# Scores of retention, attention and mLSTM computed for two heads per step, with matmuls of the two partition halves in turn

## The chip, the cores and the metric

The kernel runs on one core of a Trainium2 chip. The metric is the device time of one execution in microseconds (us). The engines are PE (matmuls, with PEld for its weight loads), DVE (vector), ACT (scalar), POOL and SP (which issues most of the large loads). PE writes its results to eight PSUM banks of 512 fp32 columns each, and the other engines read them from there.

## The reference

Two layers, each a hybrid mixer followed by an expert layer (PEER) and a gated embedding. Sequence length 512, width 1024, everything in fp32. The part that matters here is the mixer with its three groups of four heads:

```python
z = (x @ w_in)
ret = retention(q, k, v)               # 4 heads: (q k^T * decay) v, dk 64, dv 128
att = dilated_attention(q, k, v)       # 4 heads of 64: softmax with a count mask
h = mlstm(q, k, v, i, f)               # 4 heads of 64: (q k^T * exp(gates)) v / den
mix = concat(ret * silu(g), att, h * sigmoid(o)) @ w_out
x1 = layer_norm(alpha * x + mix)
y = peer(x1)                           # 16384 experts, 8 heads, top 16 rows of u and v
x = layer_norm(alpha * x1 + y + sigmoid(x1 @ wg + b) * (p @ wp))
```

For every head the scores are products of 64-long vectors. The kernel computes them in whole-sequence form: of the 512 x 512 scores of a head the lower triangle in strips of 512, 384, 256 and 128 columns.

## The kernel before

Each engine runs the same list `MIXER_STEPS` (L69) in order, taking from each step its own share; the list is written out by hand and is the order of the mixer's work on every engine. Semaphores tie the engines together, so an engine that reaches a step too early waits, and everything behind that step on its queue waits with it.

The steps of the list. `ret_qk`, `ret_v`, `att_qk`, `att_v`, `ml_qk`, `ml_vo` and `ret_g` are projections, one block of 128 tokens or columns each (`project`, L1354; `ml_qk` L1423). `ret_s`, `att_s` and `ml_s` are the scores of one head. Their shares:

- `ret_s`: PE makes the four strips (L1436) in three banks, DVE multiplies them by the decay (L1156) into `strips`.
- `att_s`: PE makes four rows of scores (L1460) in three banks: 128 and 384 columns in the first, 256 in the second, 512 in the third (`ROW_BANKS`). DVE adds the mask and takes the minimum (L1196) into `probs`, ACT takes the exponential (L696).
- `ml_s`: PE copies the gate row to all partitions with a matmul over 4 partitions (`pick`, L1479), DVE makes the exponents from it (L1227), ACT takes the exponential (L711), PE makes the strips (L1484), DVE multiplies (L1238).
- `att_tp` transposes the probabilities of a head (PE L1360, ten transposes in three banks; DVE copies them out, L1207). `ret_pv`, `att_pv`, `ml_pv` multiply with the values (L1445, L1474, L1494). After an `ml_pv` DVE divides and takes the head's statistics (L1247 to L807).
- `ml_qk`: after PE, ACT copies the block (L686), DVE convolves it (L1181, L1184), ACT applies the silu.

The q and k of head h lie in the lower 64 partitions when h is even and in the upper 64 when it is odd (`half`). So a score matmul uses one half of the array's rows, and all matmuls of one head use the same half.

`bank_turns` deals the banks: each step has a ring (0: banks 0, 1 and the two halves of `yv`; 1: banks 4, 5 and the two halves of `xps`) and a number of banks, and takes them in turn, four to a ring. `fill` makes PE wait until the previous use of that bank was read:

```python
b, turn = turns[step, i, n]
if turn > 1:
    e.wait_ge(bank_free[b], turn - 1)
```

`ret_s` and `att_s` take three banks of ring 1, `ml_s` four, `att_tp` three of ring 0, a projection one of ring 0, a `pv` one of ring 1.

## Time and profile before

| | |
|---|---|
| median of 3 runs | 3485.58 us (3484.74 to 3487.93) |
| profiled execution, its own time | 3486.61 us |
| its span in the trace | 3484.8 us |
| PE busy | 2974.9 us (85%) |
| DVE busy | 2118.6 us (61%) |
| POOL busy | 1977.5 us (57%) |
| granted clock of PE, mean | 0.972 |

The span falls into two equal layers. In each the mixer comes first (in the first layer up to about 300 us), with little DMA traffic; then the rows of the experts are gathered at around 400 GB/s.
### The profile page before, as it was taken

Reading aid. Unit: us, or ns where it says so; the run is one execution under the profiler, and the core shown is the slowest. Engines: PE = TensorE matmul, PEld = TensorE weight load, DVE = VectorE, ACT = ScalarE, POOL = GpSimd, SP = SyncE. Lnnn points to the kernel's source line nnn. Section 1 sums busy time; section 2 is a strip of 40 time slices with the busy share of each in tenths; the row PEclk is TensorE's granted clock in tenths of the full one; section 3 lists DMA queues with packets and bytes.
Section 4 is the critical chain, followed back from the end, with each engine's and each line's share of the span. In section 5 each row is a group of like instructions: output and inputs, shape, how many; then the busy total and the mean of one; then the engine's idle time right before and its main releaser. Section 6 shows DMA issues by size and latency. Waiting matters only on the chain.

```text
span 3484.8 us, 25951 instructions
## 1 busy us (share of the span) xinstructions
PE 2974.9 (85%) x7760; PEld 1319.7 (38%) x7760; DVE 2118.6 (61%) x4932; ACT 680.2 (20%) x1678; POOL 1977.5 (57%) x2100
## 2 busy tenths in 40 slices
PE   8999888888778979877799998888887799798777
PEld 4655543343223323322246555433432233233222
DVE  1435777776666666775314368776766666667753
ACT  1231211121112212121113313111111122121211
POOL 0002566667766767777400025666777667677774
PEclk9989999999999999999999899999999999999999
DMA  4114999999999999999831149999999999999997
GB/s 144 70 49 139 358 404 405 404 407 395 407 409 396 408 408 401 405 409 409 315 140 49 49 169 363 405 405 405 406 399 407 409 395 408 400 407 406 409 409 301
DMA packets 360801, 1174.44 MB, mean 337 GB/s; under 512 B 36946, under 2 KB 75986, under 8 KB 360404
## 3 DMA queue, kind: packets, MB, share of 16 engines
q0 software_dynamic: 294912, 1073.87, 78.1%
q1 hardware_dynamic: 63284, 98.59, 8.0%
q8 instruction: 62, 1.02, 0.1%
q10 hardware_dynamic: 2464, 0.31, 0.1%
q14 instruction: 79, 0.65, 0.0%
HBM read 1170.54 MB, written 2.10 MB: 336 GB/s over the span
## 4 chain that ended last, share of the span: by engine, by line
PE 41%; DMA 26%; POOL 14%; DVE 9%; issue 6%; ACT 3%; ACTq 0%; DVEq 0%; SPq 0%; POOLq 0%
DMA arena<-in_peer_v,rows 16%; PE bank L1573 12%; DMA arena<-in_peer_u,rows 9%; POOL arena L547 7%; POOL arena L556 7%; PE bank L1381 6%; DVE arena L1044 5%; PE yv L1354 5%; PE bank L1354 4%; PE bank L1534 3%; PE yv L1510 2%; ACT arena L773 1%; PE yv L1423 1%; PE bank L1510 1%; PE bank L1402 1%
## 5 line engine op out<-in xcount | busy, mean ns | idle before, releaser
L1573 PE MATMUL bank<-arena 128*128 128x512 f32 x3904 | 1884.4, 621 | 446.9 <-DMA arena<-in_peer_v,rows 390.1
L1044 DVE CUSTOM_DVE_ANT_0 arena<-arena,xps 128x1024 f32<-128x1024 f32 x1024 | 1241.4, 1216 | 589.3 <-DMA arena<-in_peer_u,rows 543.8
L1573 PEld LDWEIGHTS bank<-arena 128*128 128x128 f32 x3904 | 707.7, 194 | 1607.0 <-DMA arena<-in_peer_v,rows 924.4
L547 POOL DMA_INDIRECT arena<-in_peer_u,rows x1024 | 969.7, 947 | 499.0 <-issue 270.1
L556 POOL DMA_INDIRECT arena<-in_peer_v,rows x1024 | 970.1, 947 | 430.8 <-issue 233.6
L596 ACT ACTIVATE arena<-arena 128x16 f32<-128x16 f32 x64 | 13.9, 218 | 1874.5 <-DVE arena L1044 1874.5
L773 ACT ACTIVATE arena<-keep,arena 128x128 f32<-128x128 f32 x976 | 292.0, 387 | 39.8 <-DVE arena L1069 39.8
L1381 PE MATMUL bank<-xT,arena 128*128 128x128 f32 (+1 forms) x1024 | 229.5, 383 | 3.6 <-DMA arena<-in_peer_wq 2.1
L1381 PEld LDWEIGHTS bank<-xT,arena 128*128 128x128 f32 x1024 | 157.7, 193 | 77.6 <-issue 9.6
L1354 PE MATMUL yv<-arena,xT 128*128 128x512 f32 (+1 forms) x384 | 166.4, 588 | 0.0
L1354 PE MATMUL bank<-arena,xT 128*128 128x512 f32 (+1 forms) x384 | 159.8, 573 | 3.1 <-DMA arena<-in_w_in 2.2
L533 POOL TENSOR_TENSOR arena<-arena,normg 128x256 f32<-128x256 f32 x8 | 5.8, 725 | 193.1 <-ACTq L704 193.1
L1307 DVE TENSOR_TENSOR arena<-arena,bank 128x512 f32<-128x512 f32 x16 | 11.0, 688 | 170.1 <-ACTq L784 152.8
L1534 PE MATMUL bank<-arena,xT 128*128 128x512 f32 x256 | 112.5, 592 | 0.0
L1354 PEld LDWEIGHTS yv<-arena,xT 128*128 128x128 f32 x384 | 74.8, 200 | 80.7 <-issue 79.3
L1354 PEld LDWEIGHTS bank<-arena,xT 128*128 128x128 f32 x384 | 73.8, 195 | 82.5 <-issue 77.4
L529 POOL MEMSET arena<- 128x3 f32 x8 | 0.4, 101 | 151.1 <-PE xps L1445 151.1
L1044 DVE DVE_READ_ACCUMULATOR2_ANT arena<- 128x1 f32 x1024 | 84.6, 83 | 0.0
L1534 PEld LDWEIGHTS bank<-arena,xT 128*128 128x128 f32 x256 | 48.6, 190 | 61.2 <-issue 61.2
L1510 PE MATMUL yv<-arena,xT 128*128 128x512 f32 x160 | 69.6, 592 | 0.0
L524 POOL TENSOR_TENSOR arena<-arena 128x512 f32<-128x512 f32 x8 | 10.1, 1262 | 92.7 <-DVEq L1119 92.7
L537 POOL TENSOR_TENSOR arena<-arena,normg 128x512 f32<-128x512 f32 x8 | 10.1, 1264 | 89.7 <-ACTq L714 89.7
(289 smaller groups left out, 2007.5 us busy)
## 6 DMA issues: line engine op xcount, KB each, us to landing
arena<-in_peer_wq SPq DMA_DIRECT2D x32, 1024.0 KB, 16.5
arena<-in_w_in SPq DMA_DIRECT2D x12, 2048.0 KB, 8.7
arena<-in_peer_u,rows POOLq DMA_INDIRECT x1024, 10.7
arena<-in_peer_v,rows POOLq DMA_INDIRECT x1024, 10.8
arena<-in_w_out SPq DMA_DIRECT2D x4, 2048.0 KB, 7.9
arena<-in_ple_wg SPq DMA_DIRECT2D x4, 2048.0 KB, 21.0
arena<-in_mixer SPq DMA_DIRECT2D x2, 2112.0 KB, 19.1
ln<-in_ln SPq DMA_DIRECT2D x8, 512.0 KB, 8.2
```

Of the source, the lines that this page charges most:

```text
L547: e.indirect_dma_start(urow[i % UR], None, a["peer_u"], bass.IndirectOffsetOnAxis(ap=rows[:, n % RR, k:k + 1], axis=0)).then_inc(u_in[i % ...
L556: e.indirect_dma_start(vrow[i % VR], None, a["peer_v"], bass.IndirectOffsetOnAxis(ap=rows[:, n % RR, k:k + 1], axis=0)).then_inc(v_in[i % ...
L596: e.activation(act_d, dots[:, n % 2, :], ACT.Gelu).then_inc(gelu_done, 1)
L773: e.activation(diag[:, k, :], ident, ACT.Copy, scale=wgt[:, n % 2, k:k + 1]).then_inc(diag_ready, 1)
L1044: e.tensor_tensor_reduce(r, r, xps[:, :], 1.0, 0.0, ALU.mult, ALU.add, dots[:, n % 2, k:k + 1]).then_inc(u_free, 1)
L1354: ins = e.matmul(ps[:, 0:w], xT[:, k, i * P:(i + 1) * P], wt[:, k, :], start=(k == 0), stop=(k == KT - 1))
L1381: ins = e.matmul(ps[:, at:at + hi - lo], wq[m % 2][:, k, n * P:(n + 1) * P], xT[:, k, lo:hi], start=(k == 0), stop=(k == KT - 1))
L1402: ins = e.matmul(ps[:, b * NKEYS:(b + 1) * NKEYS], qT[:, s, b * P:(b + 1) * P], keys[m % KR][:, s, :], start=True, stop=True)
L1423: ins = e.matmul(ps[:, :], wt[:, k, i * P:(i + 1) * P], xT[:, k, :], start=(k == 0), stop=(k == KT - 1))
L1510: ins = e.matmul(ps[:, :], xT[:, k, b * P:(b + 1) * P], wt[:, k % 4, side * 512:(side + 1) * 512], start=(k == 0), stop=(k == KT - 1))
L1534: e.matmul(ps[:, :], xT[:, k, b * P:(b + 1) * P], wg[:, k, :], start=(k == 0), stop=False)
L1573: ins = e.matmul(bank[m][:, :], diag[:, k, :], vrow[i % VR][:, m * 512:(m + 1) * 512], start=(h == 0 and k == 0), stop=(h == PH - 1 and k ...
```

## The change

The scores of two heads are computed in one step. Step `ret_s`, `att_s` or `ml_s` i now stands for heads 2i and 2i+1, so there are two of each per layer and not four. Within a step PE takes a matmul of the even head (lower half of the partitions) and the same one of the odd head (upper half) in turn, each into its own bank. A pair step takes six banks (`ml_s` eight) from the same ring of four. DVE and ACT go through the pair bank by bank, first the even head and then the odd one. The amount of arithmetic is the same. The list of steps is reordered: two projections now stand between scores and their use where one did, and `att_tp` 0 and 1 (2 and 3) follow each other, as do `ret_pv` and `att_pv` of a pair and `ml_pv` 0 and 1.

```diff
-    + [("att_qk", 0), ("ret_s", 0), ("att_qk", 1), ("ret_pv", 0), ("ret_s", 1), ("att_qk", 2),
-       ("ret_pv", 1), ("ret_s", 2), ("att_qk", 3), ("ret_pv", 2), ("ret_s", 3),
-       ("att_v", 0), ("ret_pv", 3), ("att_tr", 0), ("att_tr", 1), ("att_v", 1), ("ret_norm", 0),
+    + [("att_qk", 0), ("ret_s", 0), ("att_qk", 1), ("att_qk", 2), ("ret_pv", 0), ("ret_pv", 1),
+       ("ret_s", 1), ("att_qk", 3), ("att_v", 0), ("ret_pv", 2), ("ret_pv", 3),
+       ("att_tr", 0), ("att_tr", 1), ("att_v", 1), ("ret_norm", 0),
        ("att_tr", 2), ("att_tr", 3), ("att_v", 2), ("att_v", 3), ("gate_cols", 0),
-       ("ml_qk", 0), ("att_s", 0), ("ml_qk", 1), ("att_tp", 0), ("att_s", 1),
-       ("ml_qk", 2), ("att_pv", 0), ("att_tp", 1), ("att_s", 2),
-       ("ml_qk", 3), ("att_pv", 1), ("att_tp", 2), ("att_s", 3),
-       ("ml_vo", 0), ("att_pv", 2), ("att_tp", 3), ("ml_vo", 1), ("att_pv", 3), ("ml_s", 0),
-       ("ml_vo", 2), ("ml_vo", 3), ("ml_pv", 0), ("ml_s", 1),
-       ("ret_g", 0), ("ml_pv", 1), ("ml_s", 2), ("ret_g", 1), ("ml_pv", 2), ("ml_s", 3),
-       ("ret_g", 2), ("ml_pv", 3), ("ml_norm", 0), ("ret_g", 3)]
+       ("ml_qk", 0), ("att_s", 0), ("ml_qk", 1), ("ml_qk", 2), ("att_tp", 0), ("att_tp", 1),
+       ("att_pv", 0), ("att_s", 1), ("ml_qk", 3), ("att_pv", 1), ("ml_vo", 0), ("att_tp", 2), ("att_tp", 3),
+       ("ml_vo", 1), ("att_pv", 2), ("att_pv", 3), ("ml_s", 0),
+       ("ml_vo", 2), ("ml_vo", 3), ("ml_pv", 0), ("ml_pv", 1), ("ml_s", 1),
+       ("ret_g", 0), ("ret_g", 1), ("ml_pv", 2), ("ret_g", 2), ("ml_pv", 3), ("ml_norm", 0), ("ret_g", 3)]
-    "ret_tr": (1, 1), "ret_s": (1, 3), "ret_pv": (1, 1), "att_tr": (1, 1), "att_s": (1, 3),
-    "att_tp": (0, 3), "att_pv": (1, 1), "gate_cols": (1, 1), "ml_s": (1, 4), "ml_pv": (1, 1),
+    "ret_tr": (1, 1), "ret_s": (1, 6), "ret_pv": (1, 1), "att_tr": (1, 1), "att_s": (1, 6),
+    "att_tp": (0, 3), "att_pv": (1, 1), "gate_cols": (1, 1), "ml_s": (1, 8), "ml_pv": (1, 1),
...
+            return i // 2 * 2 * NB + 2 * sum(len(js) for js in ROW_BANKS[:n]) + (1 + i % 2) * len(ROW_BANKS[n])
...
-                        if i >= 2:
-                            e.wait_ge(*step_done("att_tp", i - 2, len(ROW_BANKS) - 1))
+                        if i == 1:
+                            e.wait_ge(*step_done("att_tp", 1, len(ROW_BANKS) - 1))
                         for n, js in enumerate(ROW_BANKS):
-                            src = read(e, step, i, n)
-                            for m, (j, c) in enumerate(js):
-                                w = (j + 1) * P
-                                pr = probs[i % 2][:, ROWS_AT[j]:ROWS_AT[j] + w]
-                                e.tensor_tensor_reduce(pr, src[:, c:c + w], counts[:, SEQ - w:SEQ], -AD ** -0.5, -LOWEST, ALU.add, ALU.min, nmax[:, i, j:j + 1])
-                                e.drain()
-                                e.sem_inc(att_masked, 1)
-                            e.sem_inc(freed(step, i, n), 1)
+                            for z in range(2):
+                                src = read(e, step, i, 2 * n + z)
+                                for m, (j, c) in enumerate(js):
+                                    w = (j + 1) * P
+                                    pr = probs[z][:, ROWS_AT[j]:ROWS_AT[j] + w]
+                                    e.tensor_tensor_reduce(pr, src[:, c:c + w], counts[:, SEQ - w:SEQ], -AD ** -0.5, -LOWEST, ALU.add, ALU.min, nmax[:, 2 * i + z, j:j + 1])
+                                    e.drain()
+                                    e.sem_inc(att_masked, 1)
+                                e.sem_inc(freed(step, i, 2 * n + z), 1)
...
-                            src = read(e, step, i, 1 + n)
-                            for j, c in js:
-                                st = strips[i % 2][:, TRI_AT[j]:TRI_AT[j] + TRI[j]]
-                                done += 1
-                                e.wait_ge(ml_weight, done)
-                                ins = e.scalar_tensor_tensor(st, src[:, c:c + TRI[j]], AD ** -0.5, st, ALU.mult, ALU.mult)
-                            ins.then_inc(freed(step, i, 1 + n), 1)
-                        e.drain()
-                        e.sem_inc(ml_strip, 1)
+                            for z in range(2):
+                                src = read(e, step, i, 2 + 2 * n + z)
+                                for j, c in js:
+                                    st = strips[z][:, TRI_AT[j]:TRI_AT[j] + TRI[j]]
+                                    e.wait_ge(ml_weight, (2 * i + z) * NB + [m for m, _ in sum(TRI_BANKS, ())].index(j) + 1)
+                                    ins = e.scalar_tensor_tensor(st, src[:, c:c + TRI[j]], AD ** -0.5, st, ALU.mult, ALU.mult)
+                                ins.then_inc(freed(step, i, 2 + 2 * n + z), 1)
+                        e.drain()
+                        e.sem_inc(ml_strip, 2)
...
                         for n, js in enumerate(ROW_BANKS):
-                            ps = fill(e, step, i, n)
+                            ps = [fill(e, step, i, 2 * n + z) for z in range(2)]
                             for j, c in js:
-                                ins = e.matmul(ps[:, c:c + (j + 1) * P], half(att_qkT, 0, i, j * P, (j + 1) * P), half(att_qkT, 2, i, 0, (j + 1) * P))
-                            ins.then_inc(filled(step, i, n), 1)
+                                ins = [e.matmul(ps[z][:, c:c + (j + 1) * P], half(att_qkT, 0, 2 * i + z, j * P, (j + 1) * P), half(att_qkT, 2, 2 * i + z, 0, (j + 1) * P)) for z in range(2)]
+                            for z in range(2):
+                                ins[z].then_inc(filled(step, i, 2 * n + z), 1)
...
-                        ps = fill(e, step, i, 0)
-                        e.matmul(ps[:, :], pick[0:H, i, :], gM).then_inc(filled(step, i, 0), 1)
+                        for z in range(2):
+                            ps = fill(e, step, i, z)
+                            e.matmul(ps[:, :], pick[0:H, 2 * i + z, :], gM).then_inc(filled(step, i, z), 1)
                         e.wait_ge(ml_qkT_ready, 4)
                         for n, js in enumerate(TRI_BANKS):
-                            ps = fill(e, step, i, 1 + n)
+                            ps = [fill(e, step, i, 2 + 2 * n + z) for z in range(2)]
                             for j, c in js:
-                                ins = e.matmul(ps[:, c:c + TRI[j]], half(ml_qkT, 2, i, j * P, (j + 1) * P), half(ml_qkT, 0, i, j * P, SEQ))
-                            ins.then_inc(filled(step, i, 1 + n), 1)
+                                ins = [e.matmul(ps[z][:, c:c + TRI[j]], half(ml_qkT, 2, 2 * i + z, j * P, (j + 1) * P), half(ml_qkT, 0, 2 * i + z, j * P, SEQ)) for z in range(2)]
+                            for z in range(2):
+                                ins[z].then_inc(filled(step, i, 2 + 2 * n + z), 1)
```

The edits of `ret_s` on PE and DVE, and those of ACT's exponentials, have the same form; the waits of `att_tp` and `att_pv` on the exponentials count with `pair_rows`.

PE at the first `att_s` of a layer (`ml_qk` is L1423 before and L1432 after, `att_s` L1460 and L1470; the names in brackets are the semaphores waited for, and `bank_free` n says that bank n was read; `yv` and `xps` are two banks each). Before:

```order
L1423 MATMUL bank1<-xT,arena 128x512 [waits bank_free1,w_landed0]
L1423 MATMUL bank1<-xT,arena 128x512 x7
L1460 MATMUL bank5<-arena 128x128 [waits bank_free5,att_qkT_ready]
L1460 MATMUL bank5<-arena 128x384
L1460 MATMUL xps<-arena 128x256 [waits bank_free6]
L1460 MATMUL xps<-arena 128x512 [waits bank_free7]
L1423 MATMUL yv<-xT,arena 128x512 [waits bank_free2]
L1423 MATMUL yv<-xT,arena 128x512 x7
L1360 MATMUL yv<-keep,arena 128x128 [waits bank_free3,att_probs]
```

and now:

```order
L1432 MATMUL bank1<-xT,arena 128x512 [waits bank_free1,w_landed0]
L1432 MATMUL bank1<-xT,arena 128x512 x7
L1470 MATMUL bank5<-arena 128x128 [waits bank_free6,bank_free5,att_qkT_ready]
L1470 MATMUL xps<-arena 128x128
L1470 MATMUL bank5<-arena 128x384
L1470 MATMUL xps<-arena 128x384
L1470 MATMUL xps<-arena 128x256 [waits bank_free4,bank_free7]
L1470 MATMUL bank4<-arena 128x256
L1470 MATMUL bank5<-arena 128x512 [waits bank_free6,bank_free5]
L1470 MATMUL xps<-arena 128x512
L1432 MATMUL yv<-xT,arena 128x512 [waits bank_free2]
L1432 MATMUL yv<-xT,arena 128x512 x7
```

The step ended with the 512-column matmul into a bank of its own; now the two 512-column matmuls go into the banks that the step's first four matmuls have filled, and wait for `bank_free` of both. Two projections follow it, where one and an `att_tp` did.

PE a little later, at `att_tp` (L1360 before, L1369 now) and `att_pv` (L1474, L1483). Before, `att_pv` 0 and `att_tp` 1:

```order
L1474 MATMUL xps<-arena 128x64 [waits bank_free7,att_probsT,att_v_ready]
L1474 MATMUL xps<-arena 128x64 x9
L1360 MATMUL yv<-keep,arena 128x128 [waits bank_free3,att_probs]
L1360 MATMUL yv<-keep,arena 128x128 x3
L1360 MATMUL bank0<-keep,arena 128x128 [waits bank_free0,att_probs]
L1360 MATMUL bank0<-keep,arena 128x128
L1360 MATMUL bank1<-keep,arena 128x128 [waits bank_free1,att_probs]
L1360 MATMUL bank1<-keep,arena 128x128 x3
```

and now, `att_tp` 0 from its second bank on, `att_tp` 1 and `att_pv` 0:

```order
L1369 MATMUL bank1<-keep,arena 128x128 [waits bank_free1,att_probs]
L1369 MATMUL bank1<-keep,arena 128x128
L1369 MATMUL yv<-keep,arena 128x128 [waits bank_free2,att_probs]
L1369 MATMUL yv<-keep,arena 128x128 x3
L1369 MATMUL yv<-keep,arena 128x128 [waits bank_free3,att_probs]
L1369 MATMUL yv<-keep,arena 128x128 x3
L1369 MATMUL bank0<-keep,arena 128x128 [waits bank_free0,att_probs]
L1369 MATMUL bank0<-keep,arena 128x128
L1369 MATMUL bank1<-keep,arena 128x128 [waits bank_free1,att_probs]
L1369 MATMUL bank1<-keep,arena 128x128 x3
L1483 MATMUL xps<-arena 128x64 [waits bank_free7,att_probsT,att_v_ready]
L1483 MATMUL xps<-arena 128x64 x9
```

Both heads' transposes stand together, and the last two banks of the second head are banks 0 and 1 again, which the first head's transposes have filled.

DVE at the first `att_s` (the convolution is L1181, L1184 before and L1189, L1192 now, the masking L1196 and L1205; after each score row comes a short "ISA arena 128x1" that stores its minimum). Before:

```order
L1181 TENSOR_SCALAR arena<-arena,convw 128x512 [waits pad_filled]
L1184 SCALAR_TENSOR_TENSOR arena<-arena,convw 128x512 x3
L1196 ISA arena<-bank5,arena 128x128 [waits bank_full5]
L1196 ISA arena 128x1
L1196 ISA arena<-bank5,arena 128x384
L1196 ISA arena 128x1
L1196 ISA arena<-xps,arena 128x256 [waits bank_full6]
L1196 ISA arena 128x1
```

and now:

```order
L1189 TENSOR_SCALAR arena<-arena,convw 128x512 [waits pad_filled]
L1192 SCALAR_TENSOR_TENSOR arena<-arena,convw 128x512 x3
L1205 ISA arena<-bank5,arena 128x128 [waits bank_full5]
L1205 ISA arena 128x1
L1205 ISA arena<-bank5,arena 128x384
L1205 ISA arena 128x1
L1205 ISA arena<-xps,arena 128x128 [waits bank_full6]
L1205 ISA arena 128x1
L1205 ISA arena<-xps,arena 128x384
L1205 ISA arena 128x1
```

Up to here DVE is in the same place in both; it still convolves the block of `ml_qk` before it reads any score, and then reads four score rows of two heads, where it read two of one, before the first two banks are both free.

## Rows read from the trace of the kernel before

**Rows 1.** The page, part 4: shares of the chain that ended last.

```profile
PE 41%; DMA 26%; POOL 14%; DVE 9%; issue 6%; ACT 3%; ACTq 0%; DVEq 0%; SPq 0%; POOLq 0%
```

**Rows 2.** Stretches: us, busy us (x instructions) by engine, PEclk, DMA share, GB/s.

```profile
150.40:208.00 57.60, 57.60 (x233) 33.50 (x232) 27.67 (x71) 29.13 (x54) 1.45 (x2) 1.00 0.11 37
...
208.00:285.20 77.20, 76.41 (x217) 38.04 (x216) 28.01 (x99) 22.70 (x34) 9.03 (x8) 0.85 0.08 28
...
1945.05:2020.60 75.55, 74.72 (x217) 37.45 (x216) 27.16 (x100) 22.70 (x35) 9.04 (x8) 0.86 0.08 28
```

**Rows 3.** Timeline of PE, retention: start us, us, what, count, idle before.

```profile
87.43 1.99 PE L1436 MATMUL bank<-arena 64*128 64x512 f32 x6
...
89.78 7.13 PE L1354 MATMUL yv<-arena,xT 128*128 128x512 f32 x16
...
99.08 1.99 PE L1436 MATMUL bank<-arena 64*128 64x512 f32 x6
```

**Rows 4.** Timeline of DVE, retention scores.

```profile
89.27 1.35 DVE L1156 TENSOR_TENSOR arena<-bank,arena 128x512 f32<-128x512 f32 x3
...
100.24 0.69 DVE L1156 TENSOR_TENSOR arena<-bank,arena 128x512 f32<-128x512 f32 x1 [1.70 <-PE bank L1436]
```

**Rows 5.** Timeline of PE, attention of the first heads.

```profile
150.37 1.13 PE L1460 MATMUL bank<-arena 64*128 64x128 f32 x4
...
152.72 7.13 PE L1423 MATMUL yv<-xT,arena 128*128 128x512 f32 x16
159.69 0.60 PE L1360 MATMUL yv<-keep,arena 128*128 128x128 f32 x4
...
160.88 1.56 PE L1460 MATMUL bank<-arena 64*128 64x128 f32 x6
```

**Rows 6.** Timeline of DVE, convolution, attention scores, copies of transposes.

```profile
151.77 2.42 DVE L1184 SCALAR_TENSOR_TENSOR arena<-arena,convw 128x512 f32<-128x512 f32 x3
154.35 0.29 DVE L1196 CUSTOM_DVE_ANT_0 arena<-bank,arena 128x128 f32<-128x128 f32 x1 [0.17 <-issue]
...
154.81 0.56 DVE L1196 CUSTOM_DVE_ANT_0 arena<-bank,arena 128x384 f32<-128x384 f32 x1 [0.16 <-issue]
...
155.63 0.42 DVE L1196 CUSTOM_DVE_ANT_0 arena<-xps,arena 128x256 f32<-128x256 f32 x1 [0.25 <-issue]
...
163.70 0.76 DVE L1207 COPY arena<-yv 128x128 f32<-128x128 f32 x2
164.37 1.01 DVE L1207 COPY arena<-bank 128x256 f32<-128x256 f32 x2
```

**Rows 7.** Timelines of PE and ACT around the first `ml_vo`.

```profile
195.59 2.34 PE L1474 MATMUL xps<-arena 128*128 128x64 f32 x20
...
197.51 0.38 ACT L702 ACTIVATE arena<-yv 128x256 f32<-128x256 f32 x1
```

**Rows 8.** Timeline of PE, first `ml_s` and what follows.

```profile
208.00 1.12 PE L1479 MATMUL bank<-arena 4*128 4x512 f32 x2
...
213.36 8.52 PE L1354 MATMUL yv<-arena,xT 128*128 128x512 f32 x16
```

**Rows 9.** Timeline of DVE, first `ml_s`, first `ml_pv`, second `ml_s`.

```profile
209.16 1.68 DVE L1227 SCALAR_TENSOR_TENSOR arena<-bank,arena 128x512 f32<-128x512 f32 x4 [0.63 <-PE bank L1479]
...
232.01 0.16 DVE L1247 COPY arena<-bank 128x4 f32<-128x4 f32 x1 [18.12 <-PE bank L1494]
...
234.79 1.69 DVE L1227 SCALAR_TENSOR_TENSOR arena<-xps,arena 128x512 f32<-128x512 f32 x4
```

**Rows 10.** Stretches of low granted clock, and PE's gap before one.

```profile
209.30:216.10 6.80, 6.80 (x12) 3.00 (x12) 3.42 (x8) 1.92 (x4) 0.00 (x0) 0.50 0.00 0
...
287.80:291.20 3.40, 3.39 (x16) 3.39 (x17) 3.18 (x5) 0.58 (x1) 1.08 (x1) 0.51 0.99 408
...
287.81 1.10 PE L1360 MATMUL bank<-keep,acc 128*128 128x128 f32 x4 [2.61 <-DVE acc L1265]
```

More of the change, by code:

```diff
@@ L1220, in _ @@
                     elif step == "ml_s":
-                        if i >= 2:
-                            e.wait_ge(*step_done("ml_pv", i - 2))
-                        src = read(e, step, i, 0)
-                        for j, _ in sum(TRI_BANKS, ()):
-                            st = strips[i % 2][:, TRI_AT[j]:TRI_AT[j] + TRI[j]]
-                            ins = e.scalar_tensor_tensor(st, src[:, j * P:SEQ], -1.0, causal[:, 0:TRI[j]], ALU.mult, ALU.add)
-                            ins.then_inc(ml_expo, 1)
@@ L1240, in _ @@
-                        e.drain()
-                        e.sem_inc(ml_strip, 1)
+                        if i == 1:
+                            e.wait_ge(*step_done("ml_pv", 1))
+                        for z in range(2):
+                            src = read(e, step, i, z)
+                            for j, _ in sum(TRI_BANKS, ()):
+                                st = strips[z][:, TRI_AT[j]:TRI_AT[j] + TRI[j]]
+                                ins = e.scalar_tensor_tensor(st, src[:, j * P:SEQ], -1.0, causal[:, 0:TRI[j]], ALU.mult, ALU.add)
+                                ins.then_inc(ml_expo, 1)
+                            e.drain()
+                            e.sem_inc(freed(step, i, z), 1)
@@ new lines, in _ @@
+                        for n, js in enumerate(TRI_BANKS):
+                            for z in range(2):
+                                src = read(e, step, i, 2 + 2 * n + z)
+                                for j, c in js:
+                                    st = strips[z][:, TRI_AT[j]:TRI_AT[j] + TRI[j]]
+                                    e.wait_ge(ml_weight, (2 * i + z) * NB + [m for m, _ in sum(TRI_BANKS, ())].index(j) + 1)
+                                    ins = e.scalar_tensor_tensor(st, src[:, c:c + TRI[j]], AD ** -0.5, st, ALU.mult, ALU.mult)
+                                ins.then_inc(freed(step, i, 2 + 2 * n + z), 1)
@@ L1433, in _ @@
                         for n, js in enumerate(TRI_BANKS):
[L1434 removed]
+                            ps = [fill(e, step, i, 2 * n + z) for z in range(2)]
                             for j, c in js:
[L1436 to L1437 removed]
+                                ins = [e.matmul(ps[z][:, c:c + TRI[j]], half(ret_qkT, 2, 2 * i + z, j * P, (j + 1) * P), half(ret_qkT, 0, 2 * i + z, j * P, SEQ)) for z in range(2)]
+                            for z in range(2):
+                                ins[z].then_inc(filled(step, i, 2 * n + z), 1)
                     elif step == "ret_pv":
```

51 lines of the change are left out of this document (25 added, 26 removed).

## The prediction

> **What bounds the kernel now.** I read the chain that ended last, to see whether the mixer counts at all: PE has 41% of it [rows 1]. In the chain's order in time the mixer's pieces are PE's projections, one behind the other, and the gathers of expert rows come only after it, since they need its result. A microsecond in a mixer is one in the kernel, twice, for the two layers.
>
> Then the stretches of the mixer. In the attention part PE is busy for 57.6 of 57.6 us at the full clock, DVE for 27.7 and ACT for 29.1; in the mLSTM part for 76.4 of 77.2 us, but at a granted clock of 0.85 (second layer 0.86) [rows 2]. So PE sets the time, and less PE work would shorten it. The question is whether PE can still run without waiting: it never had to wait for a score bank.
>
> Last, single steps. Four fp32 matmuls of one head (1280 columns) take PE from 87.43 to 89.78, 2.35 us, the same in attention (150.37 to 152.72) [rows 3, 5]. Two heads in turn take 4.70. PE's work for the three mixers' scores is 12 x 2.35 = 28 us of a layer.
>
> **The change, part by part.** All durations are of the profiled execution; its own time, 3486.6 us, is 1.0 above the median of the runs.
>
> *The matmuls.* The trace of before never has matmuls of the lower and the upper half side by side, so the price of a pair is bounded: 4.70 us if they run one after the other, 2.35 plus a short tail if they overlap. I take the overlap, since the two use other rows of the array and other banks, and nothing in the rows excludes it. By this a 512-column pair takes 0.94 us and 0.4 until the second is through, a 256-column pair 0.7.
>
> The Trainium skill, page "TensorE: Matmul & The Clock Gate", section "Part 3: Packing small matmuls", has matmuls in different row groups running at once, with 3.07 times the speed for four of them. No row of this case shows it; by an estimate from that page a pair would lie at the lower of my bounds.
>
> *The banks.* A pair step fills two banks, then two more, and needs the first two again. So PE's last pair of matmuls starts only when DVE has read both of the first banks. That is the new wait, and projections are queued behind it.
>
> `ret_s` 0: PE starts at 87.43 and reaches the last pair 1.9 us later. DVE begins to read at 89.27, because it rotates `att_qk` 0 first [rows 4]; two reads of 0.69 end at 90.65. The last pair ends at 91.4: 4.0 us against 4.70. `ret_s` 1: DVE begins 1.16 after PE (100.24 against 99.08 [rows 3, 4]), is through with both banks at 2.5, PE ends at 3.3. Together **-2.1 us**.
>
> `att_s` 0: DVE convolves the projection just made before it reads a score; it reads the first 3.98 us after PE begins (154.35 against 150.37 [rows 5, 6]). The first bank of a head holds 128 and 384 columns and takes DVE 1.28 us (154.35 to 155.63). Before, PE had gone on by 152.72. Now it needs both first banks: 3.98 + 2 x 1.28 = 6.5, then the 512-column pair, 7.8 us against 4.70: **+3.1**, with PE idle for 5 us in it.
>
> `att_tp` 0 and 1: now behind `ml_qk` 2. DVE convolves that block first and copies the first transposes 4.01 us after the projection's end (163.70 against 159.69), 0.67 for the first bank (to 164.37) and 1.01 for the others [rows 5, 6]. PE makes `att_tp` 0 and the first bank of `att_tp` 1 in 1.6 us and then wants bank 0 again, which is free at 4.7, and bank 1 at 5.1. `att_pv` 0 waits for DVE's last copy of head 0, at 5.85. One `att_tp` took 1.19 (159.69 to 160.88), so it is 5.9 against 2.4: **+3.5**.
>
> `att_s` 1 has no convolution ahead: 1.16 + 2.56 = 3.7, and 1.3 for the last pair, 5.0 against 4.70: **+0.3**. `att_tp` 3 takes the bank of `ml_vo` 0, which ACT gives back when its sigmoid ends at 197.89, 2.3 us after PE's projection (195.59) [rows 7]; PE wants it at 1.15: **+1.2**. Attention in all +8.1.
>
> `ml_s` 0 at full clock: two gate rows, 1.12 each in the trace and some 0.95 when they follow each other, 1.9; DVE begins at 1.16 (209.16 against 208.00) and takes 1.68 for each head [rows 8, 9], so the banks of the gate rows are free at 4.8, where PE has waited since 3.2. Then 1.1 for the second banks, and DVE must read the first two with 0.69 each, until 6.2; end at 6.9. `ml_s` 1 has `ml_pv` 0 and 1 right before it, each 2.8 us of DVE (232.01 to 234.79 [rows 9]) while PE makes one in 2.3: DVE starts 2.3 later, end at 9.2. Together 16.1, against four steps of about 1.05 and 2.35 at full clock, 13.6.
>
> The Trainium skill, page "TensorEngine Tiling (Array Packing)", section "PSUM Bottleneck", speaks against the change in the same way: tiling speeds up TensorE but not the evacuation of PSUM. By that rule alone, with no convolution ahead of DVE, a pair of `att_s` would cost what `att_s` 1 does, +0.3; the rows ask more for `att_s` 0, since DVE is not only slow but late.
>
> *The clock.* After the 64-column matmuls of `att_pv` and the gate row the granted clock goes to 0.50 for 6.8 us and takes the projection behind (8.52 us, against 7.13) with it [rows 5, 8, 10]. Over the mLSTM part this costs 77.2 x 0.15 = 11.6 us in the first layer and 75.55 x 0.14 = 10.6 in the second. Now two such places remain in place of four. In each, about 1.8 us of matmuls and up to 2.5 us worth of projection lie at half clock, 4.3 lost; the rest falls into PE's waits. So 16.1 + 8.6 = 24.7, against 13.6 + 11.6 = 25.2 and 24.2: **about 0**.
>
> A PE gap of 2.61 us ends in 3.4 us at 0.51 [rows 10], 1.7 us lost. The gaps of 5 us in `att_s` 0 and 3.1 us in `att_tp` are new. For the first I take 2.5, between 1.7 (as in that row) and 3.4 (as 6.8 us at 0.50). Behind the second lie `att_pv` 0 with 64-column matmuls (2.34 [rows 7]), another wait of 2.1 in `att_s` 1 and then a projection; bounds are 0, if it doesn't fall, and 6.8, and I take 4.5. Together **+7.0**.
>
> *Work on other engines* (ACT's exponentials, DVE's reads, POOL's) has the same count and is costed at nothing elsewhere: PE has the projections to cover it, 6.97 us each, as before.
>
> Sum per layer: -2.1 + 8.1 + 7.0 + 0 = +13.0; for two, +26. Own time 3486.6 + 26 = 3512.6, less the 1.0: 3511.6, and I say 3511.
>
> **The rivals.**
> 1. *The halves do not overlap.* Each pair then takes its full 4.70. Where DVE sets the pace it hides part of it: retention gives back only 0.3 and not 2.1, attention loses 0.8 more, mLSTM 1.2. That is 3.8 per layer: 3519. For it: no row shows an overlap. A chance of 0.15.
> 2. *The clock stays up in attention.* The waits are there, the falls aren't: 3511 - 14 = 3497. For it: the falls shown in the mixer before came only after the gate rows and after one gap, never among `att_s` and `att_tp`. Against: gaps of 2.6 us already did it. 0.15.
> 3. *The clock stays up in the mLSTM part*, as there are half as many places and both halves work at once in them: 8.6 per layer back, 3494; with rival 2 too, 3480, no change that can be told. 0.12 and 0.04.
> 4. *Faster: PE is not held by the banks.* Six pairs at 2.2 us saved are 13 us a layer, 3459. It decides at one point: DVE must have read both first banks of a pair before PE asks for them, 1.9 us after its start. The rows have 3.2, 2.5, 6.5, 3.7 and, in mLSTM, 4.8. 0.03.
>
> **How the numbers follow.** The forecast has 0.51, and 3503 to 3519 of its own. The range takes in rival 3 below (3494) and rival 1 with both attention falls at 6.8 us, +3.2 a layer, above (3525). A measurement of this kernel tells 0.2%, 7 us, from no change. Slower by that is all above 3492.5: forecast, rivals 1 and 2 and rival 3 but for the lower part of it, 0.88; within 0.2% 0.08; faster 0.04.
>
> **What would show it.** PE's timeline must have a gap of about 5 us before the 512-column matmuls of `att_s` 0 and of 3 us inside `att_tp` 1, ended by DVE, in both layers; in `att_s` 0 the two 128-column matmuls should start apart by less than one of them takes. The attention part should grow from 57.6 to about 72 us, retention shrink by 2, mLSTM stay within 2. PEclk of the attention part should be near 0.9. The forecast is wrong if these gaps are short because DVE reads earlier than its order has it, or if the clock falls for much longer in them.

## The result and the profile after

The changed kernel takes 3504.8 us (median of 6 runs, 3500.2 to 3507.2) against 3486.1 of before (6 runs, 3484.6 to 3489.1). The ratio is 1.0049, with a 95% interval of 1.0039 to 1.0059: it is slower, by 0.5%. Its profiled execution took 3505.7 us, with a span of 3503.8 us against 3484.8, 19.0 more.

The answer to [rows 2], by stretches from the first score of attention in PE's timeline to the first gate row, and from there to the first transpose of the mixed rows. The columns are length, busy us (x instructions) of PE, PEld, DVE, ACT and POOL, PEclk, DMA share and GB/s. First the first layer's attention and mLSTM, then the second layer's attention:

```profile
147.03:220.69 73.66, 62.40 (x234) 35.47 (x233) 27.66 (x71) 25.05 (x51) 1.46 (x2) 0.86 0.08 29
220.69:295.74 75.05, 66.34 (x218) 33.68 (x217) 29.46 (x105) 17.90 (x30) 10.77 (x10) 0.89 0.10 33
1893.20:1967.21 74.01, 62.76 (x233) 35.95 (x233) 27.66 (x71) 25.05 (x51) 1.46 (x2) 0.84 0.08 29
```

Attention takes 73.7 and 74.0 us, where it took 57.6, with the same DVE work and PE idle for 11.3 us of it. The granted clock is 0.86 (0.84 in the second layer), where it was 1.00.

From the starts of steps in the two timelines:

| stretch of PE | before | after, layer 1 | after, layer 2 |
|---|---|---|---|
| first `ret_s` to first `att_tr` | 43.1, 43.1 | 40.5 | 40.5 |
| first `att_tr` to first `att_s` | 19.9, 19.9 | 19.9 | 19.9 |
| first `att_s` to first gate row | 57.6, 57.6 | 73.7 | 74.0 |
| first gate row to first `mix_tr` | 79.8, 78.1 | 75.1 | 73.1 |

Per layer this is -2.6, +16.0 and -4.8, and in the second -2.6, +16.4 and -5.0: +17.5 of the 19.0 us. The other 1.5 lie outside the mixers.

Where the time of attention goes, in PE's timeline after (start, us, what, count, and in brackets the idle time before and what ended it). These rows answer to [rows 5]; the first three show the turns:

```profile
147.03 0.37 PE L1470 MATMUL bank<-arena 64*128 64x128 f32 x1
147.04 0.37 PE L1470 MATMUL xps<-arena 64*128 64x128 f32 x1
147.24 0.27 PE L1470 MATMUL bank<-arena 64*128 64x128 f32 x1
...
153.59 1.19 PE L1470 MATMUL bank<-arena 64*128 64x512 f32 x1 [4.99 <-DVEq L1207]
...
155.60 16.17 PE L1432 MATMUL yv<-xT,arena 128*128 128x512 f32 x32
...
172.26 1.04 PE L1369 MATMUL yv<-keep,arena 128*128 128x128 f32 x8
176.50 1.21 PE L1369 MATMUL bank<-keep,arena 128*128 128x128 f32 x6 [3.20 <-DVE arena L1216]
177.50 4.43 PE L1483 MATMUL xps<-arena 128*128 128x64 f32 x20
181.86 2.08 PE L1470 MATMUL bank<-arena 64*128 64x128 f32 x8
...
186.66 2.08 PE L1470 MATMUL bank<-arena 64*128 64x512 f32 x4 [1.87 <-DVEq L1207]
188.67 8.13 PE L1432 MATMUL yv<-xT,arena 128*128 128x512 f32 x16
...
208.19 0.63 PE L1369 MATMUL yv<-keep,arena 128*128 128x128 f32 x4 [1.20 <-ACT arena L708]
```

The matmuls of the two heads start 10 ns apart: the halves run side by side. The four gaps are 4.99, 3.20, 1.87 and 1.20 us, and 4.98, 3.20, 1.87 and 1.20 in the second layer. After the first the last pair runs at half clock (1.19 us for one MATMUL of 512 columns) and the two projections take 16.01 us (155.60 to 171.61) in place of 13.84. After the second `att_pv` 0 takes 4.36 (177.50 to 181.86) in place of 2.2.

DVE at the first gap, the answer to [rows 6]:

```profile
148.43 2.42 DVE L1192 SCALAR_TENSOR_TENSOR arena<-arena,convw 128x512 f32<-128x512 f32 x3
151.02 0.29 DVE L1205 CUSTOM_DVE_ANT_0 arena<-bank,arena 128x128 f32<-128x128 f32 x1 [0.17 <-issue]
...
152.29 0.29 DVE L1205 CUSTOM_DVE_ANT_0 arena<-xps,arena 128x128 f32<-128x128 f32 x1 [0.25 <-issue]
...
153.57 0.42 DVE L1205 CUSTOM_DVE_ANT_0 arena<-xps,arena 128x256 f32<-128x256 f32 x1 [0.25 <-issue]
```

It convolves first, then reads the first bank of the even head from 151.02 and that of the odd head from 152.29, and goes on to the next bank at 153.57, when both first banks are read. PE starts the last pair at 153.59.

mLSTM, the answer to [rows 8]:

```profile
220.69 1.12 PE L1489 MATMUL bank<-arena 4*128 4x512 f32 x2
...
225.54 0.97 PE L1494 MATMUL bank<-arena 64*128 64x384 f32 x1 [1.82 <-DVEq L1239]
...
228.40 8.74 PE L1363 MATMUL yv<-arena,xT 128*128 128x512 f32 x16
...
249.41 1.12 PE L1489 MATMUL xps<-arena 4*128 4x512 f32 x2
...
256.64 0.97 PE L1494 MATMUL xps<-arena 64*128 64x384 f32 x1 [3.09 <-DVEq L1239]
...
259.50 8.55 PE L1363 MATMUL bank<-arena,xT 128*128 128x512 f32 x16
...
295.74 0.66 PE L1369 MATMUL bank<-keep,acc 128*128 128x128 f32 x4 [2.61 <-DVE acc L1274]
```

### The profile page after: what moved, and what is told of

The parts are those of the page before. It is cut to its first block, busy times and chain, and to the rows that moved or that the text cites. A ratio compares the mean times of both kernels' runs of the same rounds, so it can differ in the third digit from the quotient of the medians.

```text
span 3503.8 us, 25935 instructions
## 1 busy us (share of the span) xinstructions
PE 2963.6 (85%) x7760; PEld 1311.1 (37%) x7760; DVE 2115.1 (60%) x4932; ACT 661.4 (19%) x1664; POOL 1979.2 (56%) x2100
## 4 chain that ended last, share of the span: by engine, by line
PE 38%; DMA 29%; POOL 13%; DVE 10%; issue 6%; ACT 3%; DVEq 0%; ACTq 0%; SPq 0%; POOLq 0%
DMA arena<-in_peer_v,rows 17%; DMA arena<-in_peer_u,rows 11%; PE bank L1584 11%; POOL arena L558 6%; POOL arena L549 6%; PE bank L1390 5%; DVE arena L1051 5%; PE yv L1363 4%; PE bank L1363 4%; PE bank L1545 3%; PE yv L1521 2%; ACT arena L780 2%; PE yv L1432 1%; PE bank L1521 1%; DMA arena<-in_w_in 1%
## 5 line engine op out<-in xcount | busy, mean ns | idle before, releaser
L1363 PE MATMUL yv<-arena,xT 128*128 128x512 f32 (+1 forms) x384 | 157.5, 564 | 0.0
L1089 DVE SCALAR_TENSOR_TENSOR yv<-arena,yv 128x1024 f32<-128x1024 f32 x46 | 59.0, 1284 | 2.3 <-DMA arena<-in_peer_v,rows 1.2
## 6 DMA issues: line engine op xcount, KB each, us to landing
arena<-in_peer_wq SPq DMA_DIRECT2D x32, 1024.0 KB, 16.4
```

What stands on the lines that cost most here:

```text
L1089: e.scalar_tensor_tensor(yv[:, :], vrow[i % VR], w, yv[:, :], ALU.mult, ALU.add).then_inc(v_added, 1)
L1363: ins = e.matmul(ps[:, 0:w], xT[:, k, i * P:(i + 1) * P], wt[:, k, :], start=(k == 0), stop=(k == KT - 1))
```

## The experiments

All are made from the changed kernel or from parts of the change. Every comparison with before is with runs taken beside it; before took 3485.0 to 3487.5 us in these groups, so that a difference between two experiments, or to the changed kernel (beside which before took 3486.1), has 1 to 2 us more of doubt than the intervals say. A "stretch" is always the one of the table above.

### Each mixer's pairs alone

The edit undoes the change in the other mixers: their score steps, banks and part of the list are those of before. For retention alone, against the changed kernel:

```diff
-       ("ml_qk", 0), ("att_s", 0), ("ml_qk", 1), ("ml_qk", 2), ("att_tp", 0), ("att_tp", 1),
...
+       ("ml_qk", 0), ("att_s", 0), ("ml_qk", 1), ("att_tp", 0), ("att_s", 1),
...
-    "ret_tr": (1, 1), "ret_s": (1, 6), "ret_pv": (1, 1), "att_tr": (1, 1), "att_s": (1, 6),
-    "att_tp": (0, 3), "att_pv": (1, 1), "gate_cols": (1, 1), "ml_s": (1, 8), "ml_pv": (1, 1),
+    "ret_tr": (1, 1), "ret_s": (1, 6), "ret_pv": (1, 1), "att_tr": (1, 1), "att_s": (1, 3),
+    "att_tp": (0, 3), "att_pv": (1, 1), "gate_cols": (1, 1), "ml_s": (1, 4), "ml_pv": (1, 1),
```

> The kernel before, with the pair step and the new order for retention alone. Theory (the parts add up, each at what the stage shows in the trace after): PE's stretch from the first score of retention to the first transposes of attention goes from 43.1 to 40.5 us in each layer, and nothing else moves: 5.2 us less than before, ratio 0.9985. Rival (the reordering makes waits that only the whole set shows, or retention gains nothing by itself): ratio 1.000.

Measured: 3479.4 us, ratio 0.9980 (0.9971 to 0.9989). Retention's stretch is 40.5 us in both layers; attention's stays 57.6. The mLSTM stretch of this trace matters for what follows: its steps are those of before, and yet it is 76.4 us in both layers, where before has 79.8 and 78.1.

```profile
205.82:282.25 76.43, 73.03 (x217) 36.59 (x217) 30.28 (x105) 23.29 (x35) 10.76 (x10) 0.89 0.09 31
```

The clock is low for 17.6 and 17.4 us of it, against 23.9 and 20.5 in before (lengths worked out from the granted clock of stretches of 0.5 us). So this part moves by over 3 us per layer with nothing in it changed, and of the 7 us that this kernel gained only 5.2 are retention's for certain.

> The kernel before, with the pair step and the new order for attention alone. Theory (all of the loss is attention's, from waits of PE on score and transpose banks and the clock falls behind them): the attention stretch goes from 57.6 to about 73.8 us in each layer, 32 us more than before, ratio 1.0093. Rival (the loss is spread, or comes from the steps at the seams between the mixers): less than half of that, ratio below 1.005.

Measured: 3523.6 us, ratio 1.0108 (1.0092 to 1.0123), 37 us more. Attention's stretch is 73.7 and 72.8 us, 31 us more in all; of the rest 1 us lies in the mLSTM stretches (80.9 and 78.1), and some 3 to 5 outside the mixers.

> The kernel before, with the pair step and the new order for mLSTM alone. Theory (the gain of 4.8 us per layer that the trace after shows in the mLSTM stretch is the pair's own): 9.7 us less than before, ratio 0.9972. Rival, as the prediction had it (pair steps of mLSTM gain nothing, and the gain seen after was the luck of where the clock fell): ratio 1.000.

Measured: 3477.6 us, ratio 0.9975 (0.9966 to 0.9984). mLSTM's stretch is 74.8 and 73.4 us against 79.8 and 78.1. So the gain was no luck of one trace, and the prediction's 0 for mLSTM was wrong. Its size is less certain than these two pairs of numbers make it look: over all traces kept, the stretch is 76.4 to 80.9 us in the six layers with single heads in mLSTM (mean 78.3), and 72.5 to 75.1 in the sixteen that have pairs with the banks of one ring (mean 73.9). The two sets don't meet, and their means are 4.4 apart.

> Pair steps for retention and mLSTM, attention as before. Theory (additive): 2 x (2.6 + 4.8) = 15 us less than before, 3471 us, ratio 0.9957, faster than both kernels. Rival (the parts interfere): ratio 0.999 or more.

Measured: 3474.3 us, ratio 0.9962 (0.9949 to 0.9976), 12 us less than before and 30 less than the changed kernel. The three single parts, -7, +37 and -9, add up to +21; the whole change has +18.7. So the loss is attention's alone, within what such a comparison tells (some 5 us).

### The waits against the clock

Matmuls of no use were put where PE waits, each group into a bank that PE overwrites later; they change no result.

```diff
+            def extra(step, i, n, count):
+                ps = fill(e, step, i, n)
+                for _ in range(count):
+                    e.matmul(ps[:, :], xT[:, 0, 0:P], xT[:, 0, :])
...
+                            if n == 2:
+                                extra("ml_qk", 2 * i + 1, 0, (5, 2)[i])
...
+                            if (i, n) == (1, 1):
+                                extra("att_s", 1, 0, 3)
```

> The changed kernel, with matmuls of no use put where PE waits: five 512-column matmuls before the last pair of att_s 0, two in att_s 1 and three before the second bank of att_tp 1, each group into a bank that PE overwrites later. The waits themselves are the same length or a little less. Theory (about 8 us per layer of the loss are projections and attention matmuls at 1.2 GHz behind these gaps): the granted clock of the attention stretch stays at 1.0, 8 us per layer less, 3489 us. Rival (the clock is low because matmuls of the halves or of 64 columns keep it low, gaps or not; or it costs little, since DVE holds PE anyway): 3503 us or more.

Measured: 3489.6 us, ratio to before 1.0010 (1.0001 to 1.0019), 15 us less than the changed kernel with ten matmuls more per layer. Attention's stretch in the first layer (it is 65.6 in the second too), and pieces of it in PE's timeline (the added matmuls are L1376; five of the program show as x10):

```profile
147.13:212.70 65.57, 62.95 (x254) 34.56 (x253) 27.69 (x71) 24.94 (x51) 1.45 (x2) 1.00 0.09 33
```

```profile
148.63 4.56 PE L1376 MATMUL yv<-xT 128*128 128x512 f32 x10
153.69 0.66 PE L1478 MATMUL bank<-arena 64*128 64x512 f32 x1 [0.51 <-DVEq L1207]
...
154.75 14.00 PE L1438 MATMUL yv<-xT,arena 128*128 128x512 f32 x32
...
174.42 2.42 PE L1493 MATMUL xps<-arena 128*128 128x64 f32 x20
```

The clock stays at 1.00, the projections take 13.84 us and `att_pv` 0 2.34. PE still can't start the last pair before 153.69, 6.6 us after the step's start, as in the changed kernel. So of attention's +16.0 us, 8.1 are the clock (73.66 less 65.57), and 7.9 the waits (65.57 less 57.63), less what the pairs save in matmuls; in the second layer 8.5 and 7.9. The rival is out: neither the half-row matmuls nor those of 64 columns keep the clock low in this stretch when the gaps are filled.

### The banks

The third pair of banks of `att_s` comes from ring 0, in `bank_turns`; no order is changed.

```diff
+RINGS_OF = {"att_s": (1, 1, 1, 1, 0, 0)}
...
         for j in range(n):
+            ring = RINGS_OF.get(step, (ring,) * n)[j]
             turns[step, i, j] = (4 * ring + used[ring] % 4, used[ring] // 4 + 1)
```

> The changed kernel, with the third pair of banks of att_s taken from ring 0, so that no bank of the step is used twice in it; the order of steps is unchanged. Theory (PE waits for the first banks to be read): PE's gaps of 5.0 us in att_s 0 and 1.9 in att_s 1 are gone, and with the first of them the clock fall that costs 3.1 us; 9 to 11 us per layer less, 3484 us. Rival (DVE is the pace of the stage, and PE waits as long elsewhere, at att_tp or the next projection): 3500 us or more.

Measured: 3483.2 us, ratio to before 0.9987 (0.9978 to 0.9996); attention's stretch is 62.1 and 62.3 us. PE's rows at `att_s` 0 (the pair began at 147.98), and at `att_tp`:

```profile
149.39 1.02 PE L1474 MATMUL yv<-arena 64*128 64x512 f32 x4
150.34 14.00 PE L1436 MATMUL bank<-xT,arena 128*128 128x512 f32 x32
...
169.07 1.51 PE L1373 MATMUL yv<-keep,arena 128*128 128x128 f32 x6 [3.20 <-DVE arena L1220]
170.38 4.37 PE L1487 MATMUL bank<-arena 128*128 128x64 f32 x20
...
176.54 2.61 PE L1474 MATMUL bank<-arena 64*128 64x256 f32 x8
```

A whole pair step takes 2.36 us at full clock, what one head took before, and the gap of 5 us is gone. The gap in `att_s` 1 is gone too. That in `att_tp` stays at 3.20 and takes the clock down as before. So to take the third pair of banks of `att_s` from the step's own ring cost 21.6 us, waits and the low clock behind them together, more than the 18.7 that the whole change lost.

### The transposes

```diff
-       ("ml_qk", 0), ("att_s", 0), ("ml_qk", 1), ("ml_qk", 2), ("att_tp", 0), ("att_tp", 1),
-       ("att_pv", 0), ("att_s", 1), ("ml_qk", 3), ("att_pv", 1), ("ml_vo", 0), ("att_tp", 2), ("att_tp", 3),
-       ("ml_vo", 1), ("att_pv", 2), ("att_pv", 3), ("ml_s", 0),
+       ("ml_qk", 0), ("att_s", 0), ("ml_qk", 1), ("att_tp", 0), ("ml_qk", 2), ("att_tp", 1),
+       ("att_pv", 0), ("att_s", 1), ("ml_qk", 3), ("att_pv", 1), ("ml_vo", 0), ("att_tp", 2),
+       ("ml_vo", 1), ("att_tp", 3), ("att_pv", 2), ("att_pv", 3), ("ml_s", 0),
```

> The changed kernel, with a projection between att_tp 0 and att_tp 1, and between att_tp 2 and att_tp 3, as it was before; pairs of scores are kept. Theory (transposes of the second head wait for DVE's copies of the first): PE's gaps of 3.2 and 1.2 us there are gone, but att_s 1 now has DVE's convolution and copies ahead and waits some 2 us longer; net 2.5 us per layer less in waits, and up to 5 more if the clock stays up, 3490 to 3500 us. Rival (the new order of att_tp costs nothing, all comes from the scores' banks): within 2 us of the changed kernel.

Measured: 3494.0 us, ratio 1.0022 (1.0012 to 1.0031), 11 us less than the changed kernel. Attention's stretch is 67.5 and 68.3 us. The new place of `att_tp` costs some 6 us per layer (73.7 less 67.5, 74.0 less 68.3). The gap of 5.0 us in `att_s` 0 is still there. That of 3.20 is gone, that of 1.20 became one of 1.11 before `ml_vo` 1, and `att_s` 1 now waits 2.15 and 1.46 us in place of 1.87. The four waits are 1.5 us shorter in sum; the rest is the clock, which is low for 10.2 and 13.7 us, where it was for 20.5 and 23.9.

### DVE's lateness

```diff
-       ("ml_qk", 0), ("att_s", 0), ("ml_qk", 1), ("ml_qk", 2),
+       ("att_s", 0), ("ml_qk", 0), ("ml_qk", 1), ("ml_qk", 2),
```

> The changed kernel, with att_s 0 ahead of ml_qk 0 in the list, so that DVE reads the scores before it convolves. Theory (in att_s 0 it is mostly DVE's lateness, 3.98 us with the convolution against 1.16 without, that makes PE wait for the banks): PE's gap in att_s 0 falls from 5.0 to about 2.2 us, 2.8 us per layer less, and up to 3.1 more if the clock stays up: 3493 to 3499 us. Rival (the convolution then comes late for something else, or the gap stays since DVE's pace sets it): 3502 us or more.

Measured: 3500.9 us, ratio 1.0045 (1.0031 to 1.0058), 4 us less than the changed kernel by the medians and short of what I expected. By itself this isn't clear of noise, as the interval takes in the changed kernel's 1.0049. The traces show a gain: from the first `att_tr` to the first gate row 89.5 and 91.0 us, against 93.5 and 93.9. PE's timeline:

```profile
141.76 0.37 PE L1470 MATMUL bank<-arena 64*128 64x128 f32 x1 [1.77 <-DVEq L1171]
...
145.85 1.19 PE L1470 MATMUL bank<-arena 64*128 64x512 f32 x1 [1.75 <-DVEq L1207]
...
147.86 7.80 PE L1432 MATMUL bank<-xT,arena 128*128 128x512 f32 x16
```

The gap before the last pair is 1.75 us, but a new one of 1.77 stands before the step. It is ended by DVE's copies of the last `att_tr` (L1171), which the projection had covered. In the second layer the gap before the step is 1.97 us and that before the last pair 2.18. And the clock falls all the same, in the first layer between the two, in the second behind both. The lateness was real (5.0 to 1.75), but the projection in front also hid another wait.

### The overlap

First, all matmuls of the even head in a pair of banks, then all of the odd one:

```diff
-                                ins = [e.matmul(...) for z in range(2)]
+                            ins = [[e.matmul(...) for j, c in js][-1] for z in range(2)]
```

> The changed kernel, but within each pair of banks PE makes all matmuls of the even head and then all of the odd one, in place of turns. Theory (alternating matmuls of the two halves really run side by side): the starts of the two heads' matmuls move apart by a whole matmul, a pair of 1280 columns takes about 4.7 us of PE where DVE doesn't hold it; with the working of the first rival of the prediction, up to 3.8 us per layer more than the changed kernel, 3512 us. Rival (the halves overlap only on paper, and the order within a pair is of no weight): within 2 us of the changed kernel.

Measured: 3504.7 us, ratio 1.0053 (1.0039 to 1.0067), the same as the changed kernel. PE's rows at `att_s` 0, where the program has the 128- and the 384-column matmul of the even head (`bank`) and then the two of the odd one (`xps`):

```profile
147.48 0.37 PE L1468 MATMUL bank<-arena 64*128 64x128 f32 x1
147.50 0.37 PE L1468 MATMUL xps<-arena 64*128 64x128 f32 x1
147.69 0.27 PE L1468 MATMUL bank<-arena 64*128 64x128 f32 x1
147.71 0.27 PE L1468 MATMUL xps<-arena 64*128 64x128 f32 x1
147.81 0.48 PE L1468 MATMUL bank<-arena 64*128 64x384 f32 x1
147.82 0.48 PE L1468 MATMUL xps<-arena 64*128 64x384 f32 x1
```

The odd head's first matmul starts at 147.50, ahead of the even head's 384-column matmul at 147.81, which stands before it in the program. So the halves overlap whatever the order within the pair, and this kernel told nothing about the worth of the overlap. My expectation was wrong, and the rival's reason for it too.

So the halves were kept apart by one matmul of 4 columns over all 128 rows between them, whose result is overwritten:

```diff
+            def between(ps):
+                e.matmul(ps[:, 0:4], xT[:, 0, 0:P], xT[:, 0, 0:4])
...
+                            for z in range(2):
+                                if z == 1:
+                                    between(ps[1])
```

> The changed kernel, with the even head's matmuls of each pair of banks first, then one matmul of 4 columns over all 128 rows (its result is overwritten), then the odd head's, so that matmuls of the two halves can't run side by side. Theory (pairs overlap, but waits for DVE hide most of what that is worth): the starts of the odd head's matmuls move behind the even head's; 1 to 4 us per layer more than the changed kernel, 3507 to 3512 us. Rival (overlap sets the time of a pair step): 2.2 us for each of 6 pairs, 26 us more.

Measured: 3543.2 us, ratio 1.0167 (1.0153 to 1.0181), 38 us more than the changed kernel, well over both expectations. At the first `ret_s`:

```profile
86.70 1.12 PE L1452 MATMUL bank<-arena 64*128 64x512 f32 x2
87.76 0.39 PE L1374 MATMUL bank<-xT 128*128 128x4 f32 x2
88.07 0.69 PE L1452 MATMUL bank<-arena 64*128 64x512 f32 x1
88.08 0.91 PE L1452 MATMUL xps<-arena 64*128 64x384 f32 x2
```

The 4-column matmul takes 0.31 us of PE (87.76 to 88.07), three times per pair, some 11 us over both layers. The low clock lasts for 54.6 and 58.0 us of a mixer's attention and mLSTM stretches, against 37.6 and 41.0. That is 34 us more, which with PE busy would cost half, 17. The kernel therefore doesn't price the overlap by itself. Even here the odd head's last matmuls of one bank pair run beside the even head's first of the next (88.07 and 88.08).

### All the banks

`RINGS_OF` for the three mixers, with the order of the transposes of `tp_split`:

```diff
+RINGS_OF = {"ret_s": (1, 1, 1, 1, 0, 0), "att_s": (1, 1, 1, 1, 0, 0), "ml_s": (0, 0, 1, 1, 1, 1, 0, 0)}
```

> The changed kernel with no bank used twice within a pair step: the third pair of banks of ret_s and att_s comes from ring 0, of ml_s the gate rows and the third pair, and a projection stands between the att_tp of a pair again. Theory (the pairs are worth their overlap of 2.2 us each once PE isn't held by the banks): retention's stretch 38.5, attention's 53 to 55, mLSTM's 70 to 73 us; 14 to 17 us per layer less than before, 3452 to 3458 us, the fastest of all. Rival (DVE is the pace then, and PE waits for the strips and transposes elsewhere): 3470 us or more, no faster than the kernel with pairs in retention and mLSTM alone.

Measured: 3458.3 us (3450.3 to 3460.2), ratio to before 0.9915 (0.9902 to 0.9929). It is faster than both kernels and than `ret_ml`. Attention and mLSTM of the first layer, and PE's rows where it still waits, the last of them from the second layer:

```profile
144.44:203.55 59.11, 55.28 (x233) 31.59 (x233) 27.68 (x71) 24.83 (x51) 1.45 (x2) 0.97 0.10 36
203.55:276.13 72.58, 69.19 (x217) 35.95 (x216) 29.39 (x105) 17.91 (x30) 10.76 (x10) 0.86 0.10 33
```

```profile
88.41 0.60 PE L1449 MATMUL yv<-arena 64*128 64x256 f32 x4
88.94 14.00 PE L1367 MATMUL bank<-arena,xT 128*128 128x512 f32 x32
...
155.78 7.13 PE L1436 MATMUL bank<-xT,arena 128*128 128x512 f32 x16 [0.50 <-ACT arena L692]
...
169.41 2.13 PE L1474 MATMUL bank<-arena 64*128 64x256 f32 x8 [2.15 <-DVE acc L1230]
...
190.98 7.13 PE L1367 MATMUL yv<-arena,xT 128*128 128x512 f32 x16 [1.11 <-ACT arena L712]
...
1894.90 1.56 PE L1474 MATMUL bank<-arena 64*128 64x256 f32 x8 [2.15 <-DVE acc L1230]
```

Retention's pair takes 2.36 us (86.58 to 88.94), its stretch 38.0. Attention's stretch is 59.1 and 57.1 us and not 53 to 55. In `att_s` 1 PE waits 2.15 us in both layers, for DVE's line 1230. That line reads the bank of `att_pv` 0, and `bank_turns` gives this bank to `att_s` 1 right after it. So one wait for a bank is left, for that of another step, and DVE comes to it late, behind the convolution and the copies of `att_tp` 1 (`tp_split` has the same wait). Behind it the clock is low in the first layer (2.13 us for the matmuls, 8.2 for the projection that follows) and stays up in the second (1.56 and 7.13). mLSTM's is 72.6 and 66.0 us; the clock is low for 20.5 us of it in the first layer and for 7.3 in the second.

> all_banks with the halves kept apart by the same 4-column matmul over 128 rows. Theory: now no wait hides the overlap, and losing it costs 2.2 us for each of 6 pairs and the change of array shape on top, 13 to 18 us per layer, 26 to 36 us more than all_banks. Rival (the gain of all_banks comes from the order and the fewer changes of shape, not from the overlap): less than 10 us more.

Measured: 3502.3 us, ratio 1.0045 (1.0031 to 1.0058), 44 us more than `all_banks`. The first `ret_s` takes 4.75 us (87.82 to 92.57) against 2.36. Of these 2.4 us 0.9 are the three 4-column matmuls, and 1.5 the lost overlap and the changes of shape. As in `apart`, the odd head's matmuls of the first and the second bank pair still run beside the even head's of the next. So what this kernel takes away is a part of the overlap; it is worth some 9 us per layer or 18 in all. The added matmuls cost 11, and the rest is time at 1.2 GHz: the low clock lasts 64.9 us in the two layers' attention and mLSTM stretches against 31.2. What part of that is due to the overlap and what to the added matmuls stays open.

## Why the prediction was right or wrong

It said 3511 us, slower, and 3494 to 3525; measured are 3504.8. It was right, and by its own mechanism, but for the size of two terms. mLSTM, its largest error, took off 9.7 us over both layers where nothing was forecast; the clock in attention added 2.6, retention and the waits took off 1.4 more, and 1.5 came from outside the mixers: +26 became +19.0. That errors of both signs met made the forecast look better than its mLSTM part.

**The banks of attention: right.** The sum had +8.1 us per layer (waits, less the matmuls saved), `gaps_filled` has 7.9 in both layers. Singly: the gap in `att_s` 0 was to be 5 us and is 4.99; `att_tp` 0 and 1 with their wait were to take 5.9 and take 5.89 (171.61 to 177.50); the wait of 2.1 in `att_s` 1 is 1.87, that of 1.2 at `att_tp` 3 is 1.20.

**The clock in attention: right, a little low.** +7.0 predicted. It is 8.1 in the first layer and 8.5 in the second, by `gaps_filled` against the changed kernel's trace. Rival 2, a clock that stays up, is what `gaps_filled` made; the gaps had to be filled for it.

**Retention: right.** -2.1 predicted, -2.6 measured. The gaps before the last pairs are 1.28 and 0.67 us. The steps themselves take 3.91 and 3.30 us, as the working had it (4.0 and 3.3), and that is -2.2. The rest comes from steps of one kind that now follow each other: four `ret_pv` take 9.0 us in two pairs and took 9.2, and the projections between take 24.25 and took 24.47. The sum had no term for it.

**mLSTM: the term that was mis-sized.** "about 0" predicted, -4.8 and -5.0 measured, and `ml_only` has it alone; the sign "mLSTM stay within 2" failed with it. The full-clock part of the sum holds: the second banks of `ml_s` 0 were to start 4.8 us after the step's start and start at 4.85 (225.54 less 220.69); in `ml_s` 1 7.1 was the working (4.8 + 2.3) and it is 7.23. The step that failed is "In each, about 1.8 us of matmuls and up to 2.5 us worth of projection lie at half clock, 4.3 lost". In the first layer, from the second banks to the end takes 2.86 us in both steps, 0.8 over the 2.1 of the working and not 1.8. The projections behind lose 1.6 and 1.4 us (228.40 to 236.98 and 259.50 to 267.89, against 6.97). So some 2.3 us are lost at each place and not 4.3. In the second layer it is less still, 1.3 and 1.8 us: the same 0.8, and 0.5 and 1.0 in the projections (7.43 and 8.00 us). That is 4 and 5.5 us too many, 9.5 in all. The low clock lasts 17.1 us in the part, which would cost 8.6 with PE busy throughout; part of it falls on the waits. The two layers show that it then costs nothing: in the second the first pair of `ml_s` 0 runs at half clock (1.22 us for a MATMUL of 512 columns, against 0.69), the wait behind it is 0.86 in place of 1.82 us, and the step takes 7.72 us in place of 7.71. What it was compared with had luck in it too: the prediction took the 11.6 and 10.6 us that the clock cost in one trace of before, and in the trace of `ret_only` the same steps lose about 9.

**Overlap (rival 1): it was right to take it.** The pair takes 2.36 us, the lower of the two bounds with no tail to be seen. The rival's own price of 3.8 us per layer was not measured: `apart` has 38 us over both layers, with its added matmuls and a clock that stays low for longer.

**Rivals 3 and 4.** The clock did fall in the mLSTM part. Rival 4 named the point that decides, whether DVE has read the first banks before PE asks for them. `all_banks` took that wait away with other banks and is 27 us faster than before (3458.3 against 3485.0), as the rival had it. That the two numbers agree is in part luck, as it got there by another split: attention gains nothing (59.1 and 57.1 us against 57.6, where the rival had 4.4 less), mLSTM more (7.2 and 12.1 us).

## What to carry to other kernels

When a step is made to hold more at once, count its buffers against the ring before the engine's time: the work that it saves (2.3 us for a pair) came with a wait of up to 5 us, because the last third of the step needed banks that the reader, late by a convolution, hadn't read. The price can be read ahead from the reader's own rows: when it starts, and how long it takes for the first buffers. And a gap on PE can cost twice, once as idle time and once more as matmuls at 1.2 GHz behind it, here 7.9 and 8.1 us. The second price is small where PE would wait anyway, as in mLSTM. And a stretch in which the clock falls should be read from more than one trace: mLSTM's moved by 3 us per layer with nothing in it changed, which is more than most terms of the sum.

## What the runs showed of the hardware

Matmuls of the lower and the upper 64 partitions run side by side: 2.36 us for the 2 x 1280 columns that take 4.70 (2 x 2.35) one head after the other. The starts of the two halves don't keep the program's order, as `no_turns` shows (147.50 ahead of 147.81).

The granted clock went to 0.5 behind gaps of 4.99 and 3.20 us on PE, and stayed at 1.00 over the same stretch when the gaps held matmuls. A gap is neither needed nor enough: it fell in before with PE busy for 6.80 of 6.80 us [rows 10], and behind the same gap of 2.15 us in `all_banks` it fell in one layer and not in the other. Read in stretches of 0.5 us, it is 0.50 or 1.00 but for those in which it changes, and how much of the mLSTM part lies at the lower one changes between layers of the same execution (20.5 and 7.3 us in `all_banks`).
